# A streaming-encoder trunk in float32: where the dense operands lie in SBUF, the order of the set-up, and the lag kernels in four strips

## The reference

```python
h = rms_norm(h_res, ln_mix[i])
# layer 0: diagonal state-space mixer, 64 groups of 16 channels, 64 complex states each
bu = einsum('blgp,gnp->blgn', u, b_bar);  states = associative_scan(...)     # x_t = A x_{t-1} + B u_t
y = real(einsum('blgn,gpn->blgp', states, c_mat)) + d_skip * u
mix = (gelu(y) @ w_glu_a) * sigmoid(gelu(y) @ w_glu_b)
# layer 1: grouped-query attention, chunks of 64, window of two chunks, meta keys and sinks
mix = attention(h @ w_qkv + b_qkv) @ w_o + b_o
h_res = h_res + mix
h_res = h_res + (silu(h @ w_gate) * (h @ w_up)) @ w_down      # D_FF = 2816
out = rms_norm(h_res, ln_f)[:, 16:]
```

## Time and profile before

| | |
|---|---|
| median of 3 runs | 1266.7 us (1265.27 to 1266.8) |
| the profiled execution | 1268.77 us |
| its span, first to last instruction | 1267.0 us |
| TensorE busy, mean granted clock | 1153.2 us (91%), 0.965 |
| VectorE / ScalarE / GpSimd busy | 623.3 / 396.0 / 227.0 us |

### The profile page before, as it was taken

One profiled execution on the slowest core, in us unless ns is written; L12 is line 12 of the kernel. 1 busy time (PEld: TensorE's weight loads), 2 busy tenths in 40 slices (PEclk: granted clock), 3 DMA queues, 4 the chain that ended last, 5 costly groups with the idle time before them and its releaser, 6 DMA issues.

```text
span 1267.0 us, 19985 instructions
## 1 busy us (share of the span) xinstructions
PE 1153.2 (91%) x8083; PEld 1023.6 (81%) x8083; DVE 623.3 (49%) x907; ACT 396.0 (31%) x654; POOL 227.0 (18%) x212
## 2 busy tenths in 40 slices
PE   5256558999999999999999999999999999999997
PEld 4245447999999999999999967668888888888886
DVE  5989993445433334334444435545443343334443
ACT  5311112333322223223333345644322222223332
POOL 3788880000111211210000000000111211110000
PEclk9977778999999999999999989989999999999999
DMA  7213333223232233223223312103332223322232
GB/s 120 78 34 60 71 72 87 72 96 100 67 99 89 77 99 99 70 79 93 91 91 107 102 50 68 34 1 100 100 100 88 82 95 99 99 71 92 91 91 87
DMA packets 119513, 104.59 MB, mean 83 GB/s; under 512 B 21996, under 2 KB 117344, under 8 KB 119136
## 3 DMA queue, kind: packets, MB, share of 16 engines
q1 hardware_dynamic: 109096, 99.58, 26.3%
q10 hardware_dynamic: 10368, 4.33, 1.6%
HBM read 98.11 MB, written 5.24 MB: 82 GB/s over the span
## 4 chain that ended last, share of the span: by engine, by line
issue 43%; PE 39%; DVE 11%; POOL 3%; DMA 2%; SPq 1%; ACTq 0%; ACT 0%; POOLq 0%; DVEq 0%
PE banks L1216 37%; POOL gate L518 2%; DVE zs L1001 1%; DMA raw_c_im<-in_ssm_c_im 1%; DVE zt L1004 1%; DVE z L999 1%; DVE inj L959 1%; DVE inj_t L957 1%; DVE inj L958 1%; DVE inj_t L960 1%; PE banks L1303 0%; ACTq L610 0%; DMA y_dram<-y_act 0%; DMA y_feat<-y_dram 0%; SPq L351 0%
## 5 line engine op out<-in xcount | busy, mean ns | idle before, releaser
L540 ACT CAST w_high<-raw 128x1024 fp32r<-128x1024 f32 x188 | 197.3, 1050 | 594.9 <-PE banks L1216 594.8
L798 DVE TENSOR_TENSOR w_low<-raw,w_high 128x1024 fp32r<-128x1024 f32 x188 | 230.8, 1228 | 210.1 <-ACT w_high L540 210.0
L1216 PE MATMUL banks<-x_high,w_high 128*128 128x264 f32 (+1 forms) x1184 | 323.5, 326 | 1.0 <-DVE x_low L1031 1.0
L1216 PE MATMUL banks<-x_low,w_high 128*128 128x264 f32 (+1 forms) x1184 | 321.7, 325 | 0.0
L1216 PE MATMUL banks<-x_high,w_low 128*128 128x264 f32 (+1 forms) x1184 | 320.6, 323 | 0.0
L1216 PEld LDWEIGHTS banks<-x_high,w_high 128*128 128x128 f32 x1184 | 197.7, 189 | 21.7 <-issue 2.2
L1216 PEld LDWEIGHTS banks<-x_high,w_low 128*128 128x128 f32 x1184 | 198.8, 190 | 18.4
L1216 PEld LDWEIGHTS banks<-x_low,w_high 128*128 128x128 f32 x1184 | 198.3, 189 | 18.2
L518 POOL TENSOR_TENSOR gate<-gate,rstd_row 128x528 f32<-128x528 f32 (+1 forms) x44 | 79.3, 1802 | 396.8 <-ACT gate L678 396.8
L1216 PE MATMUL banks<-a_high,w_low 128*128 128x264 f32 (+1 forms) x528 | 140.9, 321 | 0.0
L1216 PE MATMUL banks<-a_low,w_high 128*128 128x264 f32 (+1 forms) x528 | 140.8, 321 | 0.0
(11 more groups left out here) (271 smaller groups left out, 1338.5 us busy)
## 6 DMA issues: line engine op xcount, KB each, us to landing
raw<-in_ffn_w_gate SPq DMA_DIRECT2D x22, 1024.0 KB, 5.3
raw<-in_ffn_w_up SPq DMA_DIRECT2D x22, 1024.0 KB, 5.3
raw<-in_ffn_w_down SPq DMA_DIRECT2D x16, 768.0 KB, 4.7
raw<-in_ffn_w_down SPq DMA_DIRECT2D x16, 640.0 KB, 4.4
raw<-in_attn_w_qkv SPq DMA_DIRECT2D x6, 1024.0 KB, 5.1
raw<-in_ssm_w_glu_b SPq DMA_DIRECT2D x4, 1024.0 KB, 5.2
raw<-in_ssm_w_glu_a SPq DMA_DIRECT2D x4, 1024.0 KB, 5.2
k_toep<-k_dram SPq DMA_DIRECT2D x64, 64.0 KB, 3.0
```

The lines of the kernel that those rows point to most:

```text
L540: nc.scalar.copy(w_high[:, j], raw[:, slot, :, j * P:(j + 1) * P]).then_inc(w_rounded, 1)
L798: nc.vector.tensor_tensor(w_low[:, j], raw[:, slot, :, j * P:(j + 1) * P], w_high[:, j], ALU.subtract).then_inc(w_split, 1)
L1216: ins = nc.tensor.matmul(banks[:, bank + h, 0:cn], w[:, j, k, :], xx[:, first_k + k, c0 + base:c0 + base + cn], start=start and k == 0 and ...
```

## The change

- **Place.** `w_high` and `w_low` begin on multiples of 512 bytes. Every dense operand (`glu`, `o`, `a`, `x`) is declared through `streamed`, which puts 256 bytes of padding on a multiple of 512 ahead of it, so that it begins 256 past one. The second layer's feed-forward has tiles of its own, `x1_high/low` and `a1_high/low`, with rows of 512 floats, in the same memory.
- **Parts.** 528 columns are cut into 256 and 272, put at the end of one bank and the beginning of the next, so that the two are one run of 528 in PSUM; VectorE's and ScalarE's operands on it become one run too.
- **Lags.** The four pairs of a batch go to four strips of 32 PSUM partitions (columns 0 to 127), and the skip term is added by one small matmul for each pair, so that `skip_joins` goes. `k_lag` has 128 partitions and two buffers, and is stored with one DMA, not two; `k_dram`'s order follows. VectorE waits once for `k_ready` instead of `skip_joined` ahead of the first weights that use `d_diag`'s memory.
- **Set-up.** B and C are loaded ahead of the last two pairs of token DMAs (B ahead of all), with a semaphore for each; TensorE transposes B and C ahead of the tokens. The copies to `residual` move from VectorE to ScalarE, behind all squares and ahead of `u_row`; the placing of `bbar_pair` moves to ScalarE, behind the second `u_row`. VectorE computes the powers ahead of `fine`, and the mean square behind the powers. GpSimd does `reads(0)` ahead of `coarse`. `additions(b)` waits for `u_copied`, too.

```diff
+STREAM_LINE, STREAM_SHIFT = 512, 256
+FIRST = 256
+        def streamed(name, shape, scope=ctx):
+            sb(name + "_shift", [P, STREAM_SHIFT // 4], scope=scope, align=STREAM_LINE)
+            return sb(name, shape, F32R, scope=scope)
-        w_high = sb("w_high", [P, 2, KB, P], F32R)
+        w_high = sb("w_high", [P, 2, KB, P], F32R, align=STREAM_LINE)
+        a1_high = streamed("a1_high", [P, FB, SEQ], scope=short_rows)
-        a_high = sb("a_high", [P, FB, L], F32R)
+        a_high = streamed("a_high", [P, FB, L])
...
-            return [(0, HALF), (HALF, HALF)] if n == L else [(META, SEQ)]
+            return [(0, FIRST, 512 - FIRST), (FIRST, L - FIRST, 0)] if n == L else [(META, SEQ, 0)]
...
-                sp.wait_ge(skip_joined, b + 1)
-                for j in range(2):
-                    sp.dma_start(k_dram[b, :, j, :, T - 1:, :].rearrange("q r t c -> q r (t c)"),
-                                 k_lag[j * GROUP:(j + 1) * GROUP].rearrange("q r t c -> q r (t c)")).then_inc(k_stored, 16)
+                sp.wait_ge(k_copied, b + 1)
+                sp.dma_start(k_dram[b, :, :, :, T - 1:, :].rearrange("r j q t c -> (r j q) (t c)"),
+                             k_lag[:, b % 2].rearrange("p t c -> p (t c)")).then_inc(k_stored, 16)
...
+            res_v = residual[:].rearrange("p k (c s) -> p k c s", s=T)
+            for s in range(T):
+                act.wait_ge(res_t, s + 1)
+                b0 = 2 * (s % 2)
+                nc.scalar.copy(res_v[:, :, :, s].rearrange("p (h k) c -> p h k c", h=2),
+                               banks[:, b0:b0 + 2, 0:4 * C].rearrange("p h (k c) -> p h k c", k=4)).then_inc(res_copied, 1)
             act.wait_ge(rstd0, 1)
             for i in range(5):
+                if i == 2:
+                    act.wait_ge(nat_ready, 1)
+                    act.wait_ge(pairs_cleared, 1)
+                    ...  # the four copies to bbar_pair
...
-            def skip_joins(b):
-                dve.wait_ge(k_copied, b + 1)
-                TT(k_lag[:, :, 0, :], k_lag[:, :, 0, :], d_diag[:, b * PB:(b + 1) * PB, :], ALU.add).then_inc(skip_joined, 1)
...
-                            base = 0 if xx is not o_high and xx is not o_low else -META
-                            ins = nc.tensor.matmul(banks[:, bank + h, 0:cn], w[:, j, k, :],
+                            base = -META if xx.shape[2] == SEQ else 0
+                            ins = nc.tensor.matmul(banks[:, bank + h, b0:b0 + cn], w[:, j, k, :],
...
-                for r_ in range(PB):
-                    for i in range(2):
-                        ins = nc.tensor.matmul(banks[0:2 * GROUP, 4 + b % 2, r_ * P:(r_ + 1) * P], bbar_pair[:, i, b * PB + r_, :],
+                for i in range(2):
+                    for r_ in range(PB):
+                        ins = nc.tensor.matmul(lag_rows(r_), bbar_pair[:, i, b * PB + r_, :],
                                                read[:, b % 3, i, r_, 0:T].rearrange("p t q -> p (t q)"),
                                                start=i == 0, stop=i == 1)
+                    if i == 0:
+                        for r_ in range(PB):
+                            nc.tensor.matmul(lag_rows(r_)[:, 0:GROUP], ident[0:2 * GROUP, 0:2 * GROUP], d_diag[:, b * PB + r_, :],
+                                             start=False, stop=False)
```

More of the change, by code:

```diff
@@ L498, in _ @@
             reads(0)
+            pool.wait_ge(fine_ready, 1)
+            for tab, first in ((coarse, fine[:, :, :, TA]),):
+                nc.gpsimd.memset(tab[:, 0, :, 0:1], 1.0)
+                nc.gpsimd.memset(tab[:, 1, :, 0:1], 0.0)
+                step(nc.gpsimd.tensor_copy(tab[:, :, :, 1], first))
+                k = 1
+                while k < TA:
+                    shape = [P, PAIRS, k]
+                    cmul(tab[:, 0, :, k + 1:2 * k + 1], tab[:, 1, :, k + 1:2 * k + 1], tab[:, 0, :, 1:k + 1], tab[:, 1, :, 1:k + 1],
+                         tab[:, 0, :, k:k + 1].to_broadcast(shape), tab[:, 1, :, k:k + 1].to_broadcast(shape),
+                         table_t[:, 0, :, 0:k], table_t[:, 1, :, 0:k])
+                    k *= 2
             pool.wait_ge(nat_ready, 1)
@@ L552, in _ @@
                 nc.scalar.activation(banks[0:C, 6:8, :], xt[:, s, :].rearrange("c (h n) -> c h n", h=2), ACT.Square, accum_out=mean_sq[0:C, s:s + 1]).then_inc(x_squared, 1)
+            res_v = residual[:].rearrange("p k (c s) -> p k c s", s=T)
[4 more added lines that the diff above has]
+                               banks[:, b0:b0 + 2, 0:4 * C].rearrange("p h (k c) -> p h k c", k=4)).then_inc(res_copied, 1)
             act.wait_ge(rstd0, 1)
             for i in range(5):
+                if i == 2:
+                    act.wait_ge(nat_ready, 1)
+                    act.wait_ge(pairs_cleared, 1)
+                    for j in range(2):
+                        for h, part in enumerate(("b_re", "b_im")):
+                            ins = nc.scalar.copy(bbar_pair[j * STATE:(j + 1) * STATE, h, :, j * GROUP:(j + 1) * GROUP],
+                                                 nat[part][j * STATE:(j + 1) * STATE])
+                    ins.then_inc(bbar_placed, 1)
                 if i < 4:
@@ L642, in updated @@
                 if gain != "ln_f":
-                    nc.scalar.mul(rows(x_high, m, a, e), rows(residual, m, a, e), gain_of(gain, m)).then_inc(x_rounded, 1)
+                    x_m = rows(x1_high, m, 0, SEQ) if gain == "ln_ffn1" else rows(x_high, m, a, e)
+                    nc.scalar.mul(x_m, rows(residual, m, a, e), gain_of(gain, m)).then_inc(x_rounded, 1)
                 nc.scalar.activation(square[:, a:e], rows(residual, m, a, e), ACT.Square).then_inc(squared, 1)
@@ L937, in _ @@
             dve.wait_ge(nat_ready, 1)
-            dve.wait_ge(pairs_cleared, 1)
-            for j in range(2):
-                for i, part in enumerate(("b_re", "b_im")):
-                    ins = nc.vector.tensor_copy(bbar_pair[j * STATE:(j + 1) * STATE, i, :, j * GROUP:(j + 1) * GROUP],
-                                                nat[part][j * STATE:(j + 1) * STATE])
-            ins.then_inc(bbar_placed, 1)
             def make_injection(b):
@@ L1018, in _ @@
                 if b == BATCHES - 2:
[L1019 removed]
+                    dve.wait_ge(k_ready, BATCHES)
                     split_weights(QUAD_GLU, 0)
@@ L1030, in updated @@
                     dve.wait_ge(x_rounded, k + 1)
-                    STT(rows(x_low, m, a, e), rows(residual, m, a, e), gain_of(gain, m), rows(x_high, m, a, e),
+                    high, low = (x1_high, x1_low) if gain == "ln_ffn1" else (x_high, x_low)
+                    x0, x1 = (0, SEQ) if gain == "ln_ffn1" else (a, e)
+                    STT(rows(low, m, x0, x1), rows(residual, m, a, e), gain_of(gain, m), rows(high, m, x0, x1),
                         ALU.mult, ALU.subtract).then_inc(x_split, 1)
@@ L1249, in _ @@
                 ins.then_inc(nat_tr, 1)
+            for s in range(T):
+                pe.wait_ge(x_loaded[s // 2], 32)
+                if s >= 2:
+                    pe.wait_ge(res_copied, s - 1)
+                for k in range(KB):
+                    ins = nc.tensor.transpose(banks[:, 2 * (s % 2) + k // 4, (k % 4) * C:(k % 4 + 1) * C],
+                                              xt[:, s, k * P:(k + 1) * P], ident[0:C, 0:C])
+                ins.then_inc(res_t, 1)
             pe.wait_ge(nat_copied, 3)
@@ L1401, in feed_forward @@
                             pe.wait_ge(up_taken, 2 * i + (2 * it0 + off % 2 - 1))
-                        product(QUAD_UP[layer] + i, off, 0, KB, x_high, x_low, 2 * off, n)
+                        product(QUAD_UP[layer] + i, off, 0, KB, *x, 2 * off, n)
                 def down(i):
```

172 lines of the change are left out of this document (83 added, 89 removed).

## The result

The kernel after takes 1250.16 us (median of 4 runs, 1248.1 to 1250.88), the kernel before 1265.99 us beside it (4 runs, 1263.9 to 1266.8). The ratio is 0.9874 with the interval 0.9857 to 0.9892: 16 us faster, where 33 were forecast and the range ended at 1252. The profiled execution took 1250.1 us with a span of 1247.7; against the span of before (1267.0) it is 19.3 us shorter, which is 3 us more than the medians show. Single executions of one kernel lie up to 9 us apart in this study (1229.4 to 1238.2 in e13), so single profiles are compared for their steps and medians for the sum.

The account below looks back on a forecast made before the run. TensorE bounds the dense part, mostly VectorE the batches. Layer 1's 8.7, queries' 0.5, the 528-column form's 12.4 and set-up and lags' 11.6 make 33.2 us off: median 1266.7 to 1233.5, say 1234, range 1217 to 1252.

Parts of the forecast that it names:

- Layer 1's rate: Layer 1's feed-forward: 1584 matmuls of 512 columns each 5.5 ns cheaper, at `o`'s 226.7 ns; 8.7 us off.
- Rival A: Dense products: place does nothing, only columns count, so only the 11.6 us of set-up and lags remain; 1255 us, chance 0.14.
- C: Dense products: weights on the grid remove all extra cost, 213.3 ns for 512 columns; 1174 us, half of it 1220; chance 0.06.
- The 528-column form: Dense matmuls cut into 256 + 272: 6 ns off each of 2064 pairs, 12.4 us, between bounds of 0 and 19.4.
- Rival B: Dense products: the walk of the rows keeps its price, layer 1 gains, the 528-column form nothing; 1246 us, chance 0.15.
- The upper bound: 528-column pairs at `o`'s cost per column, 0.443 ns: 233.8 ns against 243.2, at most 19.4 us off.
- Set-up and lags: Ahead of the dense part: z(0) 7.6 us earlier, four batches without `skip_joins` 2.6, last lags 1.4; 11.6 us off.
- The lags of batch 7: End of the batches: 16 records in four strips take 2.2 us instead of 3.62; 1.4 us off.
- Rival D: Set-up: strided copies on ScalarE cost twice as much and become the new wait, 8 us less gain; 1242 us, chance 0.10.
- Rival E: Dense products: the walk hits the worst phase, 528-column matmuls 3.4 ns dearer, layer 1's 6.5; 1279 us, chance 0.05.

Follow-up runs that it names:

- e13: Kernel after with rows of 576 floats, cut 264 + 264, five idle matmuls a batch, `decay_row` and small `turn`/`read` copies on ScalarE: 1232.34 us, ratio 0.9733.
- e4: Kernel before with only the places, layer 1's own tiles and the cut at 256; set-up and lags as before: 1255.42 us, ratio 0.99.
- e1: Kernel after with places, layer 1's own tiles and cut taken back, leaving the new set-up and lags: 1256.33 us, ratio 0.9898.
- m1: Separate kernel of float32r matmuls alone, varying the moving operand's place, rows and columns: 226.7 ns for 512 columns at 0 or 256 bytes.
- e2: Kernel after with the 528 columns cut into 264 + 264 instead of 256 + 272: 1248.64 us, ratio 0.9847.
- e3: Kernel after with rows of 640 floats for `x_high` and `x_low`, so that only `x` doesn't walk: 1250.05 us, ratio 0.9843.
- e10: Kernel after with rows of 576 floats for every 528-column tile and the cut 264 + 264, no idle work: 1238.66 us, ratio 0.9778.
- e6: Kernel after with idle TensorE matmuls ahead of the lags of batches 1 to 7 and in the early gated product: 1244.68 us, ratio 0.9816.
- m2: Separate kernel of matmuls alone, 256, 264 and 272 columns at 11 distances each, and pairs: best pair of 528 columns 120.0 ns a matmul.

## Why the prediction was wrong

- **Layer 1's rate, right.** 8.7 us forecast, 9.0 measured over its feed-forward, and 9.0 again with the dense part alone (e4); e1, without the dense part, keeps the old 232.2 ns. `a` gave more than the 5.5 ns assumed (232.7 to 226.7). Rival A is out, and so is C: no run went below 226.7 with the weights on the grid as well.
- **The 528-column form, the step that failed.** The prediction took 6 ns a pair, 12.4 us, because "all starts now share `o`'s 64-byte phase"; the rates in the traces give a loss of about 1.2 us instead (0.7 in layer 0's feed-forward, where matmuls went from 121.6 to 121.8 ns, and 0.5 in `glu`). The 0.7 us that layer 0's feed-forward did gain is the kernel before's stretch at the lower clock. Rival B was what happened, 1246 with everything else right. The reason given for 6 ns doesn't hold either. Half of these matmuls had `o`'s 64-byte phase before: `x` begins 224 bytes from the weights and its second half 1056 bytes further on, at 1280, a multiple of 256. And the phase of 64 bytes isn't what made `o` cheap (m1: 229 to 233 ns at 64, 128 and 192), but the distance to the weights modulo 256, and for matmuls of 256 or 264 columns even that is worth little. The upper bound was wrong in kind: it scaled `o`'s cost by columns, and a short matmul doesn't cost by columns (111 ns for 128, 120 for 256 and for 264). The most there was to gain was 121.7 - 120.06, 1.6 ns a matmul or 7 us, and it needed rows that don't walk, together with the old cut.
- **Set-up and lags, the sum right, the places not.** Forecast 7.6 + 2.6 + 1.4; by the trace up to the additions of batch 7 8.0, 2.8 (1.9 of it between batch 0 and 1, not spread over the batches) and 2.2, 13.0 in all; with the clock held up 11.0 in the medians. `skip_joins` did not make a batch 16.4 us: it is 17.56, since VectorE's other operations grew by nearly what it left. The 17.1 of the earlier trace rows was no whole batch either: from scan to scan (128.76 to 146.42) the kernel before took 17.66, so 0.1 us a batch was gained and not 0.65. The lags of batch 7 gave 2.2 where 1.4 was forecast.
- **The clock, missing from the sum.** The prediction left 0.80 as it was. With the shorter lags it went to 0.50 in this profile, `outputs(6)` took 8.4 us instead of 4.7, and 4.3 us were given back between the additions of batch 7 and layer 0, 0.5 of it by `glu`'s rate. On the kernel after, the idle work took 5.5 us off; on the version with rows of 576 floats the medians show only 0.9. The longer lags of batches 1 to 6 lay in TensorE's idle time and cost nothing there, and with them the granted clock was higher.
- **The account.** 33.2 - 12.4 (the 528-column form) - 4.3 (given back) + 1.4 (13.0 against 11.6) + 0.7 (layer 0, by the clock and not by the rate) + 0.3 (the stretch with the queries and `o`, whose own matmuls kept their rate) + 0.3 (layer 1) = 19.2, the difference of the two spans (19.3). The medians differ by 16; the 3 us between are the scatter of single executions.
- **Rival D** (dear copies on ScalarE) did not happen: 1.03 us each. **Rival E** did not either: no kind of product with 528 columns takes more than 122.5 ns a matmul in the mean. What `glu` and `a` did lose, 0.7 ns a matmul, is far from the 3.4 of that rival.

## What to carry to other kernels

Before a place in memory is given a price for one shape, measure that shape by itself: what holds for 512 columns (cheapest with a start at a multiple of 256 bytes from the weights) said nothing of pairs of 264. When work is taken from TensorE where it was idle anyway, look at the granted clock of the work behind it, and try whether idle matmuls win it back. And where VectorE and GpSimd both read SBUF all the time, a slot saved on one alone was mostly taken by longer neighbours here (0.23 us of 0.77, 0.16 of 0.91); taking from both gave 0.67.

## What the runs showed of the hardware

- In float32r with changing weights, 512 columns take 226.7 ns at a distance of 0 or 256 bytes between moving operand and weights, 229 at 64 and 320, 232 to 233 at 128, 192, 384 and 448, 237.8 at 260, at the full clock (213.3 ns would be one column a cycle; m1_rates). With both operands 128 bytes further on it is 226.9.
- Below some 264 columns the time hardly falls: 120.1 ns for 264 and 256, 112.0 for 192, 111.1 for 128 (m1_rates, the same distance for all).
- A TensorE that lost 2 us of work per batch of 17.6 in its idle time had its granted clock from 130 to 190 us fall from 0.77 to 0.50 (before and after; 0.50 to 0.83 in the profiles of e1, e2, e3 and e10); four idle matmuls a batch brought 0.63 to 0.85 back (e6).
- 256 columns alone ran at 113.5 to 113.8 ns (m1 at 192 bytes, m2 at 448) or at 117.8 (m2 at 192), at distances equal modulo 256; at the others they took 116.7 to 120.2. What decides between the two is open.
